# Down projections as Strassen's seven block products, in two sweeps over the weights

## The reference

```python
# layer 0: D_FF = 2816
h = rms_norm(x, norm_ffn[l])
gate, up = jnp.split(h @ w_gate_up[l], 2, axis=-1)
x = x + (jax.nn.silu(gate) * up) @ w_down[l]
# layers 1 and 2: D_FF_2 = 4096
h = rmsnorm(x, mlp_norm[l])
u = jnp.square(jax.nn.relu(jnp.einsum('bsd,df->bsf', h, w_ff1[l])))
x = x + jnp.einsum('bsf,fd->bsd', u, w_ff2[l])
```

## Time and profile before

| | |
|---|---|
| median of three runs | 1936.46 us |
| span of the profiled execution | 1936.4 us |
| PE busy | 1906.5 us, 98% |
| PE weight loads, beside the matmuls | 1594.4 us, 82% |
| DVE busy | 980.9 us, 51% |
| ACT busy | 810.6 us, 42% |
| POOL busy | 306.1 us, 16% |
| DMA | 167.78 MB, 87 GB/s |

### The profile page before, as it was taken

How to read it: one execution, slowest core, us unless ns; L and a number is a source line. 1 busy time by engine, 2 the same in 40 slices (tenths; PEclk the granted TensorE clock), 3 DMA queues, 4 the chain that set the end, 5 groups by cost and what they waited for, 6 DMA issues and landing times.

```text
span 1936.4 us, 24529 instructions
## 1 busy us (share of the span) xinstructions
PE 1906.5 (98%) x9718; PEld 1594.4 (82%) x9718; DVE 980.9 (51%) x1549; ACT 810.6 (42%) x1424; POOL 306.1 (16%) x378
## 2 busy tenths in 40 slices
PE   9999999999999999999999999999999999999998
PEld 7888778888888888878898888888878788888887
DVE  5566777522233357589842233337668962223334
ACT  4445876422223235277533232223547743323222
POOL 2133344000000010003412220001002312221000
PEclk9999999999999999999999999999999999999999
DMA  7212111233333322221133333332121224333331
GB/s 240 57 56 93 55 44 45 90 103 93 96 97 98 98 79 65 87 88 45 54 120 98 98 96 93 96 96 89 55 88 44 70 73 125 94 98 96 98 98 55
DMA packets 97138, 167.78 MB, mean 87 GB/s; under 512 B 8160, under 2 KB 49152, under 8 KB 97024
## 3 DMA queue, kind: packets, MB, share of 16 engines
q1 hardware_dynamic: 97024, 166.21, 27.6%
HBM read 164.09 MB, written 2.10 MB: 86 GB/s over the span
## 4 chain that ended last, share of the span: by engine, by line
PE 86%; DVE 5%; ACT 4%; POOL 2%; issue 2%; DMA 0%; SPq 0%; DVEq 0%; POOLq 0%; ACTq 0%
PE ps L49 83%; PE ps L52 3%; DVE wlo L71 2%; ACT sk1h L65 1%; POOL p L71 1%; ACT whi L65 1%; ACT p L62 1%; ACT L62 1%; DVE p L91 1%; POOL hTl L71 1%; DMA raw<-in_w_in_dram 0%; DVE pS L91 0%; DVE rot L71 0%; DVE hTl L71 0%; DVE x L71 0%
## 5 line engine op out<-in xcount | busy, mean ns | idle before, releaser
L65 ACT ACTIVATE whi<-raw 128x1024 fp32r<-128x1024 f32 (+1 forms) x294 | 310.0, 1054 | 728.2 <-PE ps L49 725.0
L71 DVE TENSOR_TENSOR wlo<-raw,whi 128x1024 fp32r<-128x1024 f32 (+1 forms) x294 | 361.0, 1228 | 395.1 <-ACT whi L65 392.1
L49 PE MATMUL ps<-hTh,whi 128*128 128x512 f32 (+1 forms) x1176 | 442.3, 376 | 0.0
L49 PE MATMUL ps<-hTh,wlo 128*128 128x512 f32 (+1 forms) x1176 | 437.7, 372 | 0.0
L49 PE MATMUL ps<-hTl,whi 128*128 128x512 f32 (+1 forms) x1176 | 437.6, 372 | 0.0
L49 PE MATMUL ps<-whi,uh 128*128 128x512 f32 x688 | 268.0, 390 | 0.0
L49 PE MATMUL ps<-whi,ul 128*128 128x512 f32 x688 | 267.7, 389 | 0.0
L49 PE MATMUL ps<-wlo,uh 128*128 128x512 f32 x688 | 267.6, 389 | 0.0
L49 PEld LDWEIGHTS ps<-hTh,wlo 128*128 128x128 f32 x1176 | 220.8, 188 | 39.8
L49 PEld LDWEIGHTS ps<-hTh,whi 128*128 128x128 f32 x1176 | 221.0, 188 | 37.1 <-DVE wlo L71 0.4
L49 PEld LDWEIGHTS ps<-hTl,whi 128*128 128x128 f32 x1176 | 221.1, 188 | 36.4
(11 more groups left out here) (243 smaller groups left out, 2290.4 us busy)
## 6 DMA issues: line engine op xcount, KB each, us to landing
raw<-in_w_ff_dram SPq DMA_DIRECT2D x128, 512.0 KB, 3.6
raw<-in_w_gate_up_dram SPq DMA_DIRECT2D x88, 256.0 KB, 3.1
raw<-in_w_in_dram SPq DMA_DIRECT2D x40, 512.0 KB, 4.6
raw<-in_w_in_dram SPq DMA_DIRECT2D x68, 256.0 KB, 3.1
raw<-in_w_down_dram SPq DMA_DIRECT2D x22, 512.0 KB, 3.5
raw<-in_w_o_dram SPq DMA_DIRECT2D x16, 512.0 KB, 4.3
x<-in_x_dram SPq DMA_DIRECT2D x8, 512.0 KB, 6.5
raw<-in_w_out_dram SPq DMA_DIRECT2D x8, 512.0 KB, 3.9
```

Source lines behind the costliest of these rows:

```text
L49: return self.eng.matmul(out, l, r, start=start, stop=stop, skip_group_check=True)
L65: return self.eng.activation(out, in_, ACT.Copy)
L71: return self.eng.tensor_tensor(out, a, b, op)
```

## The change

Two neighbouring feature tiles (256 features) times both halves of the tokens (256 each) times both halves of the output columns (512 each) are a product of 2 x 2 blocks: K is two tiles, and so are rows and columns. Done directly this is eight block products, 48 matmuls of 128 x 512. The change does it by Strassen's seven, 42 matmuls. Each of the seven multiplies a block or a sum of blocks of the tokens with a block or a sum of blocks of the weights. Each of them is accumulated in PSUM over all pairs of feature tiles and is added to (or subtracted from) one or two quarters of x at the end. A product takes two banks (`r` = 0, 1, a block of 128 tokens each); seven would take fourteen banks, so there are two sweeps:

- sweep A, products M4, M1, M6, M3: over all 16 (layer 0: 11) pairs, eight banks, 24 matmuls a pair. A pair takes two weight units; POOL, DVE and POOL again make the sums of blocks in place in `raw` (`weight_sums`, `weight_difs`, `weight_sums_2`) before the split. The token side has two tiles a pair: two plain blocks (`u_hi`) and two differences that POOL makes in `udif` (`token_difs`).
- sweep B, products M5, M7, M2: the weights are read again, as units of one 128 x 512 block from each of two pairs (in layer 0 one pair is left over and goes alone), 12 matmuls a unit, three units for two pairs. POOL makes one sum in `raw` (`block_sums`) and the differences of tokens in place in `u` (`token_blocks`).

In SBUF the two `htmp` buffers become the third pair of `raw` buffers while a down projection runs (six in all, taken as three pairs in sweep A); `whi` and `wlo` stay at four. `DB` assigns banks, `BEFORE` names whose bank a product of sweep B takes over; its first matmul waits until DVE has added that bank to x. `down_add` has 24 instructions a layer. The last two pairs of sweep A are taken product by product, the last three units of sweep B in the order (a,0) (b,0) (a,1) (b,1) (c,0) (c,1). The order on the engines comes from a planner run (`plan_down`, started 16 us ahead of the end of the up projection) in place of a formula.

```diff
-        U["dn", m] = rows(w_ff2_2[m - 1], 32) if m else rows(w_down[0], 22)
+        w_d, nk = (w_ff2_2[m - 1], 32) if m else (w_down[0], 22)
+        U["dn", m] = row_pairs(w_d, nk)
+        U["dB", m] = row_blocks(w_d, nk)
...
+    def sums_of(M, r):
+        return {"M4": [(r, 0, 1), (2 + r, 0, 1)], "M1": [(r, 0, 1), (2 + r, 1, 1)], "M6": [(2 + r, 1, -1)],
+                "M3": [(r, 1, 1), (2 + r, 1, 1)], "M5": [(r, 0, 1), (r, 1, -1)], "M7": [(r, 0, 1)],
+                "M2": [(2 + r, 0, 1), (2 + r, 1, -1)]}[M]
...
+            P.add(("raw", j), "SP", 0.3, *raw_after(m, j), seq="raw", lat=4.2)
+            P.add(("wsA", k), "POOL", 2.05, ("raw", i), ("raw", i + 1), seq="ws", pri=2)
+            P.add(("wsB", k), "DVE", 0.64, ("wsA", k), seq="wsB", pri=0)
+            P.add(("wsC", k), "POOL", 1.18, ("wsB", k), seq="wsC", pri=1)
+            split(i, ("wsB", k))
+            split(i + 1, ("wsC", k))
...
+            P.add(("udf", k), "POOL", 1.18, *ready, ("ul", (m, "s", p - 2)) if p >= 2 else None, seq="udf", pri=3)
...
+            for p, M, r in pairs_order(m):
+                second = M in ("M6", "M3")
+                unit, b = U["dn", m] + 2 * p + second, DB[m][M][r]
+                pe.wait_ge(*at("wlo", unit))
+                pe.wait_ge(*at("ul", (m, "s" if M in ("M6", "M1") else "r", p)))
...
+                for a, c in P3:
+                    ins = pe.mm(ps[b][:, :], st[a][:, c0:c0 + 128], (whi, wlo)[c][unit % NS][:, w0:w0 + 512], ...)
...
+        def weight_difs(m):                            # DVE, sweep A, 128 x 512
+                dve.tt(q[:, 3, :], q[:, 0, :], q[:, 3, :], ALU.subtract)
+        def weight_sums(m):                            # POOL, sweep A, 128 x 1024
+                pool.tt(q[:, 1:3, :], q[:, 1:3, :], q[:, 3::-3, :], ALU.add)
+        def weight_sums_2(m):                          # POOL, sweep A, 128 x 512
+                pool.tt(q[:, 0, :], q[:, 3, :], q[:, 1, :], ALU.add)
+        def token_difs(m):                             # POOL, sweep A, 128 x 512
+                pool.tt(udif[p % 2][:, :, :], bc(u[:, 2 * p, 0:256], 1, [128, 2, 256]), u[:, 2 * p:2 * p + 2, 256:512], ALU.subtract)
+        def block_sums(m):                             # POOL, sweep B, 128 x 1024, once in three units
+                    pool.tt(raw[RS[i]][:, 0:512 * k], raw[RS[i]][:, 0:512 * k], raw[RS[i - 1]][:, 0:512 * k], ALU.add)
+        def token_blocks(m):                           # POOL, sweep B, 128 x 1024 and 128 x 512, once in three units
+                    pool.tt(v[:, :, 0, :], v[:, :, 0, :], v[:, :, 1, :], ALU.subtract)
+                    pool.tt(v[:, :, 1, 0:256], v[:, :, 1, 0:256], v[:, :, 1, 256:512], ALU.subtract)
```

More of the change, by code:

```diff
@@ L246, in decoder_program @@
     r = Region(RAW0, SP0)
-    raw = [r.t("raw%d" % i, [128, 1024]) for i in range(NR)]
+    quads = [r.t("raw%d" % i, [128, 4, 512]) for i in range(NR // 2)]
     r = Region(SP0, TMP0)
@@ L257, in decoder_program @@
     gtmp = [r.t("gtmp%d" % i, [128, 512]) for i in range(3)]
+    udif = [r.t("udif%d" % i, [128, 2, 256]) for i in range(2)]
     r = Region(X0, U0)
@@ L383, in decoder_program @@
                 cols(w_gate_up[0], [(256 * g, 256), (2816 + 256 * g, 256)])
-        U["dn", m] = rows(w_ff2_2[m - 1], 32) if m else rows(w_down[0], 22)
+        w_d, nk = (w_ff2_2[m - 1], 32) if m else (w_down[0], 22)
+        U["dn", m] = row_pairs(w_d, nk)
+        U["dB", m] = row_blocks(w_d, nk)
+        U["end", m] = len(plan)
+    RS, RP, W_HT = {}, {}, {}
+    latest = {j: j - 10 for j in range(6)}
+    for i in range(len(plan)):
+        m = next((m for m in range(3) if U["dn", m] <= i < U["end", m]), None)
+        if m is not None and i < U["dB", m]:
+            if (i - U["dn", m]) % 2 == 0:
+                pair = min(range(3), key=lambda j: max(latest[2 * j], latest[2 * j + 1]))
+                RS[i], RS[i + 1] = 2 * pair + 1, 2 * pair
+        else:
+            RS[i] = min(range(6 if m is not None and i < U["end", m] - 4 else 4), key=lambda j: latest[j])
+        RP[i] = latest[RS[i]] if latest[RS[i]] >= 0 else None
+        latest[RS[i]] = i
+        if RS[i] >= 4:
+            W_HT[m] = i
     CH = 1.36
@@ new lines, in raw_after, with k_of, y_of @@
+    def raw_after(m, i):
+        after = [("wlo", RP[i])] if RP[i] is not None else []
+        after += [("wsC", k_of(RP[i]))] if k_of(RP[i]) else []
+        after += [("ysm", y_of(RP[i]))] if y_of(RP[i]) else []
+        return after + [("up", m, 1, 0, 0)] * (RS[i] >= 4)
+    def k_of(i):
+        for m in range(3):
+            if i is not None and U["dn", m] <= i < U["dB", m] and (i - U["dn", m]) % 2 == 0:
+                return m, (i - U["dn", m]) // 2
+    def y_of(i):
+        for m in range(3):
+            if i is not None and U["dB", m] <= i < U["end", m] and (i - U["dB", m]) % 3 == 0:
+                return m, i - U["dB", m] + 1
@@ L960, in totals, with summed, u_pair, u_block @@
         return hf[:, h, 256 - (1024 >> lv):256 - (512 >> lv)]
+    def summed(i):
+        for m in range(3):
+            if U["dn", m] <= i < U["dB", m]:
+                p, second = divmod(i - U["dn", m], 2)
+                return ("wsC" if second else "wsB"), (m, p)
+            if U["dB", m] <= i < U["end", m] and (i - U["dB", m]) % 3 == 1:
+                return "ysm", (m, i - U["dB", m])
+        return None
+    def u_pair(m, p):
+        v = u[:, 2 * p:2 * p + 2, :].rearrange("p k (c n) -> p (k c) n", c=2)
+        return v[:, 0:4:3, :]
+    def u_block(m, n):
+        _, M, p, k = list(units_b(m))[n]
+        v = u[:, 2 * p:2 * (p + k), :].rearrange("p (a k) n -> p a k n", k=2)
+        return v[:, :, 1 if M == "M7" else 0, 256:512] if M == "M2" else v[:, :, 1 if M == "M7" else 0, 0:256]
+    def us_view(s, part, n):
+        return us[s][part][:, 0:256 * n].rearrange("p (c n) -> p c n", c=n)
     def sp_program(sp):
```

345 lines of the change are left out of this document (265 added, 80 removed).

## The result

The changed kernel takes 2212.05 us (median of 4 runs, 2211.1 to 2214.67), the one before 1937.07 beside it: ratio 1.142, 95% interval 1.1404 to 1.1437. The direction was right, the size was not: +275 us where +71.5 was forecast, and 2212 lies above the range (1955 to 2070).

What follows compares the result with a forecast made beforehand. PE's instruction stream bounded the kernel; afterwards DVE and POOL taking turns would. Down projections +67.0 us and ends +4.5 made +71.5 on 1936.4, so 2008 us; range 1955 to 2070 over all cases, the forecast's own 1972 to 2075.

Steps and rivals of the forecast that it cites:

- PE's gain: Down projections: 6 matmuls less in each of 43 pairs, 258 x 0.227 = 58.5 us.
- The exclusion: Both sweeps: DVE and POOL instructions reading two SBUF tiles exclude each other, so times add: 7.96 us a pair in sweep A.
- handover: Point in the weight-sum chain where the next engine isn't waiting yet, so 0.15 us is exposed.
- Rival 1: Down projections: DVE and POOL work beside each other, PE stays the bound; -51 us, 1885 us, chance 0.12.
- the turns: Both sweeps: DVE and POOL alternate, each instruction costing its time less about 0.15 us that overlaps the other's.
- POOL's prices: POOL's sums in both sweeps: 2.2 us for 1024 columns, 1.18 us for 512.
- The ends: Two layer borders and the kernel's end: PE stands some 1.5 us at each, 4.5 us in all (1 to 9).
- I take one such in each cycle: Both sweeps: one exposed 0.15 us handover per cycle, giving 8.1 us in A and 10.2 in B.
- Rival 4: Down projections: fixed list order starves DVE and adds count in full; +33 us, 2040 us, chance included in the forecast's.
- rival 3: Sweep A: PE's clock falls after long waits, 9.3 us a pair instead of 8.1; +52 us, 2060 us, chance 0.10.
- The adds at nothing: DVE's 24 instead of 8 adds a layer, 11 us more each, run beside POOL's turns and cost nothing.
- the sum without any overlap: Both sweeps at full DVE and POOL durations, cycles of 9.4 and 11.7 us: +160 us, 2096 us.

Runs made afterwards that it cites:

- e1: Changed kernel with the planner's down-weight loads chained on issue instead of landing; same instructions, only their order in the lists differs: 2096.8 us, ratio 1.083.
- e5: Changed kernel with all of POOL's block sums moved to DVE, planned jointly as in e4: 1957.0 us, ratio 1.011.
- e9: e4 with each POOL sum replaced by fills of about equal length that read nothing (sums not computed): 1963.2 us, ratio 1.013.
- e4: Changed kernel with only its plan changed: e1's edit, POOL's sums planned on DVE's time, due times as priorities: 2088.9 us, ratio 1.079.
- e8: e5 with the steps of the next layer's norm planned first: 1960.1 us, ratio 1.012.
- e7: e4 with the matmuls of high tokens by low weights left out of the down projections: 2072.1 us, ratio 1.07.

## Why the prediction was right in sign and wrong in size

- **PE's gain, right.** 258 matmuls fewer, 58.5 us; sweep B's 8.16 us in e1, e5 and e9 shows that it can be had where nobody else limits. In sweep A e9's steady pair takes 5.95 us, 5.44 only at the start.
- **The exclusion, right, as mechanism and as size.** Sum 7.96 us a pair, or 8.1 with a handover; e4 runs at 8.47, of which 0.34 is POOL's price. Rival 1 (PE stays the bound, 1885) fell: e4 shows the turns, and even without the exclusion e9 comes to 1963.
- **POOL's prices, too low.** I took 2.2 and 1.18 us; they are 2.36 and 1.27, the upper ends I had. By the forecast's own sum this gives cycles of 8.45 and 10.6 us and +91 in the place of +67.
- **The ends, too low.** 4.5 us (1 to 9) forecast, 20 measured (9.0, 9.1 and 3.8 behind layers 0, 1 and 2, less 1.7 ahead of the first down projection), and 21 in e5. The lower clock behind PE's waits there wasn't in the sum. The extra addition and the queue behind the last matmul were named, but priced as if nothing else were in DVE's list; the border rows under e8 show what is.
- **"I take one such in each cycle": the step that failed.** One exposed handover of 0.15 us stood for all that the lists do. It is true of sweep A in e4, whose order was planned for the turn-taking. In the order of the change a pair takes 10.8 us and three units 12.0. Rival 4 (the fixed order starves DVE) named the mechanism and gave it, together with the adds in full, 33 us. That is the price of the adds alone (3 x 11), so the order stood in the sum at nothing; it is worth 123. It was priced on a false premise, "the planner's times assume 5.44 us a pair"; by the code they assume 0.3 + 4.2 us a unit in one chain, 9.0 us a pair. I asked what is ready, and not whom each list puts ahead of the next thing PE needs. I also took each sweep's sums to be made in that sweep, and the lists put sweep B's token differences into sweep A.
- **PE's clock (rival 3), right in kind.** It was given +52 as a case apart. It came together with the waits: some 75 us of the 724, where before showed one of two stretches. In the other orders less of it is left, 46 us in e1, 30 in e4 and 14 in e5, and not in proportion to the waits (150 us of them in e1, 157 in e4).
- **The adds at nothing.** That they take no part in the turns is so: 12 adds of the changed kernel and 23 of e4 ran beside one of POOL's sums for more than 0.3 us, and all took 0.67 to 0.68 us; three of POOL's 1024-column sums that met nothing but adds took 2.37 to 2.41 us, those that met nothing at all 2.34 to 2.40. What their own time costs in DVE's list wasn't tried. In e5, where DVE is full in sweep A, they can't be free.
- **The range.** Its top, 2070, lay below two numbers of the same text: the 2075 of the forecast's own range and the 2096 of the sum without any overlap. 2212 is above all three.

From the forecast's +71.5 to the 273.7 of the spans (rounded terms, 274): POOL's prices +24, the ends +15.5, what e4 has beyond that +40 (not taken apart; its layer 1 has uneven periods in sweep B and a wait of 7.6 us near the end of sweep A), the order +123 (2210.1 - 2087.4).

## What to carry to other kernels

When work moves to engines with lists written ahead, read the plan's own pace before pricing the instructions: a latency that sits in a chain, instead of beside it, sorts every list for a kernel that doesn't exist. Look in each list for an instruction that waits for the end of a product standing ahead of one that feeds the next product. And in this kernel POOL was no second DVE for sums of two SBUF tiles: it was 132 us slower to share them than to give all to DVE.

## What the runs showed of the hardware that I had not expected

- The clock doesn't follow the length of the waits alone. In sweep A of layer 1, e4's PE waits 40 us in 37 pieces, e7's 55 us in 43 pieces, both a good 1 us in the mean; e4's granted clock is 0.96, e7's 0.81:

```profile
1181.40:1313.90 132.50, 85.28 (x258) 56.57 (x256) 121.22 (x77) 49.98 (x64) 108.37 (x50) 0.81 0.40 127
```

  The rows differ in the matmuls between the waits, 258 in place of 386, and in the 15 us more of waits. Which of them decides was not tried.
- A POOL instruction of two inputs costs about twice DVE's for the same tile (2.36 against 1.22 us, 1.27 against 0.68), and a fill of it less than half of the sum's time (0.95 and 0.53 us).
- Filling POOL with 5.0 us a pair of write-only work beside DVE stretched none of DVE's low parts by more than 0.01 us (e9, layer 1's sweep A: 1.216 to 1.227 us and 0.683 to 0.693).
